# The first norm worked out on the tokens as they come in, and the residual stream turned between the products of the first units

## The reference, cut to what matters

```
def rms_norm(x, g):
    xf = x.astype(F32)
    y = xf * lax.rsqrt(jnp.mean(xf * xf, axis=-1, keepdims=True) + NORM_EPS)
    return (y * g.astype(F32)).astype(x.dtype)
...
h = rms_norm(x, norm_mix[0])
z, xbc, dt_raw, q, k, v = split_cols(h @ w_in, EVEN_SIZES)
x = x + even_mixer(...)
```

## Time and profile before

| | |
|---|---|
| median of 3 runs (lowest to highest) | 3689.18 us (3687.64 to 3690.46) |
| the profiled execution's own time | 3688.5 us |
| its span, first to last instruction | 3686.6 us |
| busy: PE, PEld, DVE, ACT | 95%, 77%, 50%, 35% of the span |
| mean granted TensorE clock | 0.972 |
| first product of first_units starts | 28.78 us |
| next products after them start | 54.29 us |

### The profile page before, as it was taken

How to read it: one execution, slowest core, us unless ns; L and a number is a source line. 1 busy time by engine, 2 the same in 40 slices (tenths; PEclk the granted TensorE clock), 3 DMA queues, 4 the chain that set the end, 5 groups by cost and what they waited for, 6 DMA issues and landing times.

```text
span 3686.6 us, 43526 instructions
## 1 busy us (share of the span) xinstructions
PE 3488.2 (95%) x17636; PEld 2853.4 (77%) x17636; DVE 1861.7 (50%) x2957; ACT 1295.2 (35%) x2206; POOL 104.9 (3%) x144
## 2 busy tenths in 40 slices
PE   8988888999987899999999998999999999999997
PEld 6656668888865688888888866888888888788886
DVE  6664676443676354335434535643364436564434
ACT  4442434222453332224222443422242225543223
POOL 0000000000100000000000100100010001010001
PEclk9999999999988999999999999999999999999998
DMA  3102112223310122232233211222322232013231
GB/s 121 55 26 74 58 47 83 96 97 106 96 53 1 40 98 97 97 103 98 97 99 103 84 49 46 81 97 97 103 86 97 97 109 72 30 47 114 97 103 63
DMA packets 89146, 296.65 MB, mean 80 GB/s; under 512 B 15726, under 2 KB 17524, under 8 KB 88948
## 3 DMA queue, kind: packets, MB, share of 16 engines
q1 hardware_dynamic: 85784, 290.24, 23.5%
q10 hardware_dynamic: 3164, 3.64, 0.3%
HBM read 291.61 MB, written 2.10 MB: 80 GB/s over the span
## 4 chain that ended last, share of the span: by engine, by line
PE 79%; DVE 13%; ACT 5%; issue 2%; POOL 0%; DMA 0%; ACTq 0%; DVEq 0%; POOLq 0%
PE ps L296 23%; PE ps L298 23%; PE ps L297 23%; PE ps L293 10%; DVE XT L666 1%; ACT WH L278 1%; DVE WL L284 1%; DVE mb_cv L1542 1%; DVE XL L672 1%; PE ps L2459 1%; DVE R L576 0%; ACT od_p L2062 0%; POOL XT L447 0%; DVE S L585 0%; DVE od_t L2254 0%
## 5 line engine op out<-in xcount | busy, mean ns | idle before, releaser
L296 PE MATMUL ps<-XH,WH 128*128 128x512 f32 (+1 forms) x3200 | 1187.9, 371 | 41.2 <-DVE XL L672 25.9
L297 PE MATMUL ps<-XL,WH 128*128 128x512 f32 (+1 forms) x3200 | 1173.8, 367 | 0.0
L298 PE MATMUL ps<-XH,WL 128*128 128x512 f32 (+1 forms) x3200 | 1173.4, 367 | 0.0
L284 DVE TENSOR_TENSOR WL<-RAW,WH 128x1024 fp32r<-128x1024 f32 x548 | 664.2, 1228 | 298.7 <-ACT WH L278 295.7
L296 PEld LDWEIGHTS ps<-XH,WH 128*128 128x128 f32 x3200 | 608.9, 190 | 150.3 <-DVE XL L672 19.1
L298 PEld LDWEIGHTS ps<-XH,WL 128*128 128x128 f32 x3200 | 608.8, 190 | 98.0
L297 PEld LDWEIGHTS ps<-XL,WH 128*128 128x128 f32 x3200 | 609.2, 190 | 96.4 <-issue 1.7
L278 ACT ACTIVATE WH<-RAW 128x1024 fp32r<-128x1024 f32 x548 | 565.4, 1049 | 87.0 <-PE ps L293 60.1
L296 PE MATMUL ps<-HH,WH 128*128 128x512 f32 (+1 forms) x1188 | 435.2, 366 | 0.0
L297 PE MATMUL ps<-HL,WH 128*128 128x512 f32 (+1 forms) x1188 | 434.1, 365 | 0.0
L298 PE MATMUL ps<-HH,WL 128*128 128x512 f32 (+1 forms) x1188 | 434.1, 365 | 0.0
(11 more groups left out here) (560 smaller groups left out, 3233.2 us busy)
## 6 DMA issues: line engine op xcount, KB each, us to landing
RAW<-units SPq DMA_DIRECT2D x548, 512.0 KB, 3.3
XIN<-in_x ACTq DMA_DIRECT2D x2, 1024.0 KB, 6.3
out<-OUT SPq DMA_DIRECT2D x4, 512.0 KB, 2.6
da_pi<-in_positions ACTq DMA_DIRECT2D x1, 256.0 KB, 3.0
mb_pairf<-constants ACTq DMA_DIRECT2D x1, 256.0 KB
wa_dist<-constants ACTq DMA_DIRECT2D x1, 192.0 KB, 2.9
da_lb<-in_ev_lambdas ACTq DMA_DIRECT2D x1, 128.0 KB, 2.9
od_bin<-in_od_b_im SPq DMA_DIRECT2D x1, 128.0 KB, 3.2
```

What stands on the lines that cost most here:

```text
L284: nc.vector.tensor_tensor(WL[:, u % RING, :], RAW[:, u % RING, :], WH[:, u % RING, :].bitcast(F32), ALU.subtract)\
L296: nc.tensor.matmul(out, wh, xh, start=start, stop=False)
L297: nc.tensor.matmul(out, wh, xl, start=False, stop=False)
L298: return nc.tensor.matmul(out, wl, xh, start=False, stop=stop)
```

## The change

The stage n_mix0 goes; stage load takes its work over, and does it on the token-major input, where the sum of squares of a token is a sum along a row.

- ACT squares each of the four 128 x 1024 token blocks as its transfer lands, with the sum of each row as a by-product (`squares`, `accum_out`).
- PE turns `VROW` at once, before anything of x; DVE copies it to `VEC`.
- DVE works out the scales of a half on 128 x 2 numbers (`scales`: one instruction, and `rsqrt`, a bit trick of two instructions and three Newton steps of three; twelve small instructions, each waiting for the one before) and multiplies the half's two token blocks by them, 128 x 1024 each, into a new buffer `XN`.
- PE turns `XN` tile by tile (two blocks for a k); ACT (`high`) writes XH from PSUM, with the gain as scale; DVE (`low`) writes XL from the same PSUM and XH. The steps of R, XT, S2, the sums on PE and the roots on ACT aren't there any more.
- Half 0 is done so before the first products. DVE's order in it: low(0), low(1), low(2), WL of units 0 and 1, low(3), low(4), scales(1), low(5), WL of unit 2, low(6), low(7). ACT's order: high(0), high(1), WH of units 0 and 1, high(2) to high(4), WH of unit 2, high(5) to high(7).
- Half 1 is turned inside `first_units`: after the nine products of each k, PE turns two blocks of `XN` of half 1 (bank 6 or 7) and four blocks of the raw `XIN` into bank 4 or 5 (`tokens_turned`), from which ACT copies tile k of `R`, 128 x 512. The splits of units 3 to 5 follow high and low of k = 1, 3, 5. The sums of half 1 on PE at k = 4 are gone.
- Later norms count their roots and sums from one less (`e["sc"]`), and the output's turns from 24.

`_STAGES` begins "load ev_attn" where it began "load n_mix0 ev_attn". The diff, cut to its core:

```diff
+        XN = sb("XN", [P, TT, D], at=WORK + 16 * KB)
+        xs = sb("x_scales", [P, 3, TT], at=WORK2 + 10 * KB)
...
-        TAIL = dict(load=8, ffn=1, ev_attn=0, ev_mamba=3, od=3, win=3, mlstm=3)
-        r_count = sq_count = add_count = tail_count = norm_count = f_count = nr_count = 0
+        TAIL = dict(ffn=1, ev_attn=0, ev_mamba=3, od=3, win=3, mlstm=3)
+        sq_count, r_count = 2, 0
+        add_count = tail_count = norm_count = f_count = nr_count = 0
...
+            elif kind == "load":
+                e["c"], norm_count, nr_count = 0, 1, KD
-                e["c"], e["prod"], e["nr0"] = norm_count, prod, nr_count
+                e["c"], e["sc"], e["prod"], e["nr0"] = norm_count, norm_count - 1, prod, nr_count
...
-                if k == 4:
+                if nrm["kind"] == "load":
+                    tokens_turned(pe, k)
+                elif k == 4:
                     stats_pe(pe, nrm, 1)
...
+            if nrm["kind"] == "load":
+                pe.wait_ge(S["norm_r"], KD)
+        def tokens_turned(pe, k):
+
+            if k == 0:
+                pe.wait_ge(S["xt_ready"], 2)
+            pe.wait_ge(S["x_ready"], KD + k - 1)
+            for j in range(2):
+                last = nc.tensor.transpose(ps[:, 6 + k % 2, j * P:(j + 1) * P], XN[:, 2 + j, k * P:(k + 1) * P], ident[:])
+            last.then_inc(S["turned"], 1)
+            if k >= 2:
+                pe.wait_ge(S["norm_r"], k - 1)
+            for j in range(TT):
+                last = nc.tensor.transpose(ps[:, 4 + k % 2, j * P:(j + 1) * P], XIN[:, j, k * P:(k + 1) * P], ident[:])
+            last.then_inc(S["turned"], 1)
...
-            nxt["behind"] = e if e["kind"] == "norm" else e.get("behind")
+            nxt["behind"] = e if e["kind"] in ("norm", "load") else e.get("behind")
...
             def load(e):
-                for q, (k, h) in enumerate(e["tiles"]):
-                    if k == 0:
-                        pe.wait_ge(S["x_in1" if h else "x_in0"], 16)
-                    if q >= 2:
-                        pe.wait_ge(S["r_ready"], q - 1)
+                pe.wait_ge(S["vrow_in"], 16 * sum(ap is not None for ap, _, _ in vrows))
+                for a, b in vec_pages():
+                    last = nc.tensor.transpose(ps[:, 0, a:b], VROW[0:b - a, a // P, :], ident[0:b - a, 0:b - a])
+                last.then_inc(S["vec_ready"], 1)
+                pe.wait_ge(S["xt_ready"], 1)
+                for k in range(KD):
+                    if k >= 2:
+                        pe.wait_ge(S["x_ready"], k - 1)
                     for j in range(2):
-                        last = nc.tensor.transpose(ps[:, 6 + q % 2, j * P:(j + 1) * P], XIN[:, 2 * h + j, k * P:(k + 1) * P], ident[:])
+                        last = nc.tensor.transpose(ps[:, 6 + k % 2, j * P:(j + 1) * P], XN[:, j, k * P:(k + 1) * P], ident[:])
                     last.then_inc(S["turned"], 1)
-                    if (k, h) == (KD - 1, 0):
-                        pe.wait_ge(S["vrow_in"], 16 * sum(ap is not None for ap, _, _ in vrows))
-                        for a, b in vec_pages():
-                            last = nc.tensor.transpose(ps[:, 0, a:b], VROW[0:b - a, a // P, :], ident[0:b - a, 0:b - a])
-                        last.then_inc(S["vec_ready"], 1)
-                    if (k, h) == (1, 1):
-                        stats_pe(pe, e["norm"], 0)
...
-                    act.wait_ge(S["var_ready"], 2 * e["c"] + h + 1)
+                    act.wait_ge(S["var_ready"], 2 * e["sc"] + h + 1)
...
+            def load(e):
+
+                def squares(h):
+                    act.wait_ge(S[f"x_in{h}"], 16)
+                    for j in (2 * h, 2 * h + 1):
+                        last = nc.scalar.activation(XN[:, j, :], XIN[:, j, :], ACT.Square, accum_out=xs[:, 0, j:j + 1])
+                    last.then_inc(S["sq_ready"], 1)
+
+                def high(k, h):
+                    act.wait_ge(S["turned"], KD + 2 * k + 1 if h else k + 1)
+                    nc.scalar.activation(XH[:, k, HALVES[h]], ps[:, 6 + k % 2, 0:HT], ACT.Copy, scale=vcol("norm_mix", k))\
+                        .then_inc(S["xh_ready"], 1)
+
+                squares(0)
+                squares(1)
+                act.wait_ge(S["vec_ready"], 2)
+                for k in range(KD):
+                    high(k, 0)
+                    if k in (1, 4):
+                        hi_to(act, 2 if k == 1 else 3)
+                for k in range(KD):
+                    high(k, 1)
+                    act.wait_ge(S["turned"], KD + 2 * k + 2)
+                    nc.scalar.activation(R[:, k, :], ps[:, 4 + k % 2, :], ACT.Copy).then_inc(S["norm_r"], 1)
+                    if k in (1, 3, 5):
+                        hi_to(act, 4 + (k - 1) // 2)
+
...
-                    tail_act(act, e, 0)
+                    load(e)
...
-            def load_half(h):
-                def go(e):
-                    for q in range(8 * h, 8 * h + 8):
-                        dve.wait_ge(S["turned"], q + 1)
-                        finish(e, q, ps[:, 6 + q % 2, 0:HT], None)
-                return go
-
-            second = dict(load=load_half(1), ffn=ffn_tail(1))
+            second = dict(ffn=ffn_tail(1))
 
             def load(e):
-                load_half(0)(e)
+                def scales(h):
+
+                    ms, y, a = (xs[:, i, 2 * h:2 * h + 2] for i in range(3))
+                    dve.wait_ge(S["sq_ready"], h + 1)
+                    own(v.tensor_scalar(ms, ms, 1.0 / D, RMS_EPS, ALU.mult, ALU.add))
+                    rsqrt(own, ms, y, a)
+                    for j in range(2):
+                        own(v.tensor_scalar(XN[:, 2 * h + j, :], XIN[:, 2 * h + j, :], y[:, j:j + 1], None, ALU.mult),
+                            "xt_ready" if j else None, wait=j == 1)
+
+                def low(k, h):
+                    dve.wait_ge(S["xh_ready"], KD * h + k + 1)
+                    own(v.scalar_tensor_tensor(XL[:, k, HALVES[h]], ps[:, 6 + k % 2, 0:HT], vcol("norm_mix", k),
+                                               XH[:, k, HALVES[h]].bitcast(F32), ALU.mult, ALU.subtract), "x_ready")
+
                 dve.wait_ge(S["vec_ready"], 1)
                 for n, (a, b) in enumerate(vec_pages()):
-                    own(v.tensor_copy(VEC[:, a:b], ps[:, 0, a:b]))
-                lo_to(dve, 3)
+                    own(v.tensor_copy(VEC[:, a:b], ps[:, 0, a:b]), "vec_ready" if n == len(vec_pages()) - 1 else None)
+                scales(0)
+                for k in range(KD):
+                    low(k, 0)
+                    if k == 2:
+                        lo_to(dve, 2)
+                    if k == 4:
+                        scales(1)
+                    if k == 5:
+                        lo_to(dve, 3)
+                for k in range(KD):
+                    low(k, 1)
+                    if k in (1, 3, 5):
+                        lo_to(dve, 4 + (k - 1) // 2)
+                dve.wait_ge(S["norm_r"], KD)
...
-        load=dict(kind="load"), store=dict(kind="store"),
-        n_mix0=dict(gain=("norm_mix", 0), **RMS), n_ffn0=dict(gain=("norm_ffn", 0), **RMS),
+        load=dict(kind="load", gain=("norm_mix", 0)), store=dict(kind="store"),
+        n_ffn0=dict(gain=("norm_ffn", 0), **RMS),
...
```

More of the change, by code:

```diff
@@ L186, in build @@
         ffn_act ffn_dve r_ready sq_ready s2_added stats_ready
-        var_ready root_ready t_ready xh_ready x_ready x_in0 x_in1 turned out_ev norm_r ln_scaled""".split()
+        var_ready root_ready t_ready xh_ready x_ready x_in0 x_in1 turned xt_ready out_ev norm_r ln_scaled""".split()
         S = {n: sem(n) for n in names}
@@ L245, in build @@
                 r_count += len(e["tiles"])
-                tail_count += e["tail"] if kind != "load" else 0
+                tail_count += e["tail"]
                 e["sums"] = e["tail"] > 0
@@ L258, in build @@
                     f_count += 1
-                e["x"] = norm_count - 1
+            elif kind == "load":
+                e["c"], norm_count, nr_count = 0, 1, KD
             elif kind == "norm":
-                e["c"], e["prod"], e["nr0"] = norm_count, prod, nr_count
+                e["c"], e["sc"], e["prod"], e["nr0"] = norm_count, norm_count - 1, prod, nr_count
                 prod["norm"] = e
@@ L526, in norm @@
                         root(1)
-                    act.wait_ge(S["t_ready"], 16 * e["c"] + t + 1)
+                    act.wait_ge(S["t_ready"], 16 * e["sc"] + t + 1)
                     g = vcol(e["gain"][0], e["gain"][1] * 8 + k)
@@ L540, in norm @@
                         hi_to(act, nx + {5: 4, 10: 5, 13: 6}[t])
+            def load(e):
[21 more added lines that the diff above has]
+                        hi_to(act, 4 + (k - 1) // 2)
             def outs(a, z):
                 for q in range(a, z):
-                    act.wait_ge(S["turned"], 16 + q + 1)
+                    act.wait_ge(S["turned"], 24 + q + 1)
```

(6 more changed lines are left out.)

## The result

The kernel became slower by 0.15%: medians 3694.43 us (3691.54 to 3697.5, 22 runs) against 3688.94 us (3687.55 to 3692.79, 22 runs), ratio 1.0015 [1.0009, 1.0021]. That is +5.5 us, with an interval of 3.3 to 7.7, and inside the 0.2% that I had called no measurable difference. The forecast was 3693.1 in 3687 to 3698. The profiled execution took 3693.75 us with a span of 3691.6 (before 3688.5 and 3686.6), mean granted clock 0.973 (before 0.972).

What follows compares the result with a forecast made beforehand. DVE was taken to bound the head up to the first product, PE from there. Start -0.5, turns +5.3 and removed sums -0.87 gave +3.9 us, a forecast median of 3693.1 us, range 3687 to 3698.

Steps and rivals of the forecast that it cites:

- The path: First 54 us: DVE bounds up to the first product at 28.78 us, then PE to 54.29 us with nothing to fill.
- The start: First product, set by DVE's queue: at 28.25 us against 28.78, 0.5 us earlier; bounds 26.8 to 29.8.
- VROW's landing: Head of DVE's queue: the gains' transfer taken to land at 8.8 us, copies to VEC done at 10.3.
- the second stall: DVE before low(2): idle 2.1 us while ACT does WH of units 0 and 1 ahead of high(2).
- The turns: PE between the first products: 48 added turns at 0.11 us each, +5.3 us.
- the four sums of -0.87: PE at k = 4: four matmuls of sums of half 1 go, saving 0.87 us.
- ACT as the bound between the products: Rival: gaps or slower reads from PSUM make ACT set the pace there, +1.2 to +4 us; chance 0.12.
- A clearly earlier start: Rival: first product at 23.9 to 26.8 us, time 3687 to 3691; chance 0.16 including a start before 17.
- The clock low through eight rounds: Rival, 28 to 54 us: turns among products keep PE at half speed, +10 us, time 3703 to 3705; chance 0.06.
- The term of 0 to 1.1 us more: Start of the products: half-speed stretch of up to 5.5 us instead of 3.3, costing up to 1.1 us more.
- Later stages do the same work in the same order: After the head: the rest adds no difference, so the sum of +3.9 us carries to the end.
- a difference behind 60 us unlike that at 58 us: Named sign of being wrong: the shift after 60 us differs from that where products on WH start, expected at 58.2 us.

Runs made afterwards that it cites:

- scale_first: Changed kernel with the scales and multiplication of half 0 placed before the copies to VEC; median 3690.85 us, ratio 1.0006 to the kernel before.
- r_twice: Changed kernel with R's four turns of each k made twice, 32 more turns among the products; median 3694.33 us, ratio 1.0016 to the kernel before.
- r_early: Changed kernel with all of R's 32 turns made before the first product; median 3691.19 us, ratio 1.0006 to the kernel before.
- wh_first: Changed kernel with WH of units 0 and 1 before ACT's first XH; median 3693.65 us, ratio 1.0013 to the kernel before.
- head_reordered: Changed kernel with its head reordered (scales before VEC, WH first, half 1 later, 36 turns in the stream); median 3683.07 us, ratio 0.9985 to the kernel before.
- after_again: The changed kernel itself, unchanged, measured once more in a later batch; median 3694.52 us, ratio 1.0015 to the kernel before.
- before_turns: Kernel before with 48 unread turns added, six after each k's products; median 3692.15 us, ratio 1.001 to the kernel before.
- r_thrice: Changed kernel with R's turns made three times, 64 more turns; median 3700.45 us over 6 runs, ratio 1.0032 to the kernel before.
- busy_turns: Changed kernel with 33 useless turns in PE's idle time before the first product; median 3690.65 us, ratio 1.0005 to the kernel before.
- busy_again: Unchanged repeat of busy_turns in a later batch; median 3689.92 us, ratio 1.0005 to the kernel before.

## Why the prediction was right

By its own steps:

- **The path.** Right. DVE up to the first product, PE without a break from there to the landmark, nothing to hide the turns. scale_first moves the first by DVE's order alone, r_twice and r_early the second by turns alone.
- **The start, -0.5 forecast, +0.06 measured.** The mis-sized term is VROW's landing: 10.2 where I took 8.8. I had put its last packets at 8 to 8.25 us, and in the changed kernel the first turn's wait ended 2 us after that; this profile doesn't tell what filled those. The small steps (0.20 each) and the squares (1.06) were right; two multiplications took 1.42 for my 1.55, so the scaled tokens came at 15.15 for my 14.25. Of the 0.9 the second stall gave back 0.5 (1.60 for my 2.1), and of that stall ACT's WH, which I had made the whole cause, is only half (wh_first). The start came 0.6 later than forecast, and the gain of 0.5 wasn't there at all.
- **The turns, +5.3 forecast.** 48 x 0.107 = 5.1; the four sums of -0.87 gone with them, the stretch from first product to landmark should grow by 4.3 and grew by 4.39 (29.90 against 25.51). The price taken from four turns at 285 us held; the switch to and from turns is in both prices.
- **ACT as the bound between the products** (rival). Wrong: PE has no idle time there. A copy of the tokens to XH took 0.46 (counted as 0.51) and one of R 0.60, as counted, and there is space between:

ACT's timeline of the changed kernel in the stream:

```profile
39.10 0.46 ACT L570 ACTIVATE XH<-ps,VEC 128x256 fp32r<-128x256 f32 x1
39.46 0.60 ACT L583 ACTIVATE R<-ps 128x512 f32<-128x512 f32 x1
...
40.67 0.47 ACT L570 ACTIVATE XH<-ps,VEC 128x256 fp32r<-128x256 f32 x1 [0.62 <-PE ps L360]
```

- **A clearly earlier start** (rival). It didn't come of itself, since both stalls and VROW were there. scale_first and head_reordered show that it was to be had, by DVE's order.
- **The clock low through eight rounds** (rival, the other side). Wrong: 3.55 us in both kernels. The term of 0 to 1.1 us more was needed, though: over the kernels without added busy turns the stretch was 3.07 to 6.10 us, and 4.83 in after_again, the same program, whose landmark is 0.66 later. I had priced a slow stretch at half its length; by the pitches it is 0.44 of it, which is the same in both kernels and drops out.
- **"Later stages do the same work in the same order", at no change.** True of the work; of the time, +4.45 at the landmark stands against +5.5 [3.3, 7.7] in the medians, which agree only within the interval. Of the 1.6 us by which +5.5 misses the forecast of +3.9, the landmark shows 0.55 (4.45 for 3.9), which is the start's; the other 1.0 is no step of the sum. That the median fell so near the forecast is in part luck: an offset like that of r_twice would have moved it by some 3 us. Three groups of instructions, each in the kernel before and then in the changed one (first and last start behind the lengths), show the shift within the profiled executions:

```profile
L297 PE MATMUL ps<-da_yl,WH x64: 387/389/628, 244.7 to 340.8; 128*128 128x512 f32 x64
...
L297 PE MATMUL ps<-mb_yl,WH x88: 280/283/628, 530.7 to 594.2; 128*128 128x256 f32 x48, 128*128 128x512 f32 x40
...
L2459 PE MATMUL ps<-ident,wa_p x160: 270/272/332, 3121.3 to 3245.6; 128*128 128x128 f32 x160
```

```profile
L301 PE MATMUL ps<-da_yl,WH x64: 387/389/632, 247.7 to 343.0; 128*128 128x512 f32 x64
...
L301 PE MATMUL ps<-mb_yl,WH x88: 277/283/628, 534.8 to 598.0; 128*128 128x256 f32 x48, 128*128 128x512 f32 x40
...
L2524 PE MATMUL ps<-ident,wa_p x160: 270/272/332, 3127.5 to 3251.7; 128*128 128x128 f32 x160
```

The shift is +3.0 and +2.2 at 245 and 341 us, +4.1 and +3.8 at 531 and 594, +6.2 and +6.1 at 3121 and 3246, +5.0 at the end. It wanders by up to 4 us along one pair of executions, though the work is the same. The prediction had named a difference behind 60 us unlike that at 58 us as a sign of being wrong; that sign is there, and the repeats showed that a part of it belongs to each program. In the profiled executions the time from landmark to last instruction is 3628.6 to 3633.8 us over all kernels, and in the two of the change 3632.9 and 3630.1, so one execution's share is large too. Where the slow stretches of the clock fall is what I suspect. The granted clocks speak for it only in part: averaged over a kernel's runs they are highest in before_turns and r_twice (0.9745 and 0.9743), whose times fall furthest short of their heads, and lowest in r_early (0.9717), whose time doesn't; but r_thrice has 0.9742 and falls short by 0.5 only. None of the runs isolates it, so the cause of this offset is open.

## What to carry to other kernels

Ask of each moved step which engine is the bound at its new place. The 32 turns of R cost nothing while DVE was the bound and 3.4 us under the products. When work is split so that the first half can start early, keep the second half's steps out of the queue ahead of the first product, and don't let an engine's first instruction wait for a transfer that its next ones don't need. A head's landmark tells cleanly what an edit does there; the end of a 3.7 ms kernel may differ from it by 2 to 3 us, repeatably, so an edit of that size is judged at the landmark and claimed only there.

## What the runs showed of the hardware

- Turns alone, f32 128x128, brought the array to its full clock: 16 took 3.62 us in r_early at 10.46 and 1.91 in busy_turns at 23.43. In r_early, with 22 turns behind it, the first four of XN took 0.66 us (the second line of its timeline); the same four in the change, with only the two of VROW behind them, took 1.11:

```profile
15.20 1.11 PE L486 MATMUL ps<-ident,XN 128*128 128x128 f32 x4 [4.38 <-DVE XN L662]
```

- After the busy turns came an idle gap of 2.15 us in one run and 2.16 in the other, and the full clock was lost by the first product in the one (busy_turns) and kept in the other (busy_again). PE's timeline of busy_again at that gap:

```profile
27.27 0.44 PE L486 MATMUL ps<-ident,XN 128*128 128x128 f32 x2 [2.16 <-DVE XL L669]
```

- The column of the granted clock can't be read at the start of a program before its first fall. In ten of the thirteen traces it stands at 1.00 in every window ahead of 32 us, also where products of 128x256 follow each other at 0.213 us; there the pitch tells the clock. In r_early, busy_turns and head_reordered the column falls to 0.50 at about 17.7, 27.7 and 18.1 us (estimates from windows of 1 us) and agrees with the pitch from there on. Windows of busy_turns, PE alone (busy, clock, DMA share, GB/s):

```profile
24.00:27.00 3.00, 1.34 (x13) 1.00 0.00 0
...
28.00:31.00 3.00, 2.73 (x13) 0.50 0.00 0
```

- Three programs kept their distances from the kernel before to within 0.5 us in two batches each, though these distances differ from those of their heads by up to 2.8 us.
